# Row scales of the two MLPs: TensorE matmuls and a ScalarE copy, or a write to scratch memory and a broadcast read

## What is computed

```python
def rms_norm(x, g):
    xf = x.astype(jnp.float32)
    y = xf * lax.rsqrt(jnp.mean(xf * xf, axis=-1, keepdims=True) + EPS)
    return (y * g.astype(jnp.float32)).astype(x.dtype)

def squared_relu_mlp(h, w_up, w_down):
    a = jax.nn.relu(h @ w_up)
    return (a * a) @ w_down

# for each layer l: first the mixer, then
        x = x + squared_relu_mlp(rms_norm(x, mlp_norm[l]), w_up[l], w_down[l])
```

## Time and profile before

| | us |
|---|---|
| median of 3 runs (1101.26 to 1101.33) | 1101.28 |
| the profiled execution, its own time | 1101.01 |
| its span in the trace | 1099.2 |
| PE busy | 1091.1 (99%) |
| DVE busy | 782.8 (71%) |
| ACT busy | 479.4 (44%) |
| POOL busy | 77.3 (7%) |
| share of the DMA engines in weight loads (queue 1) | 31.4% |

### The profile page before, as it was taken

The page is one execution under the profiler, slowest core; times in us unless marked ns, Lnnn a source line. Parts: engine busy times, 40 slices in busy tenths (PEclk is TensorE's granted clock), DMA queues, the critical chain, the costliest instruction groups (busy, mean ns, idle before and its releaser), DMA issues.

```text
span 1099.2 us, 13443 instructions
## 1 busy us (share of the span) xinstructions
PE 1091.1 (99%) x5168; PEld 900.2 (82%) x5168; DVE 782.8 (71%) x980; ACT 479.4 (44%) x695; POOL 77.3 (7%) x58
## 2 busy tenths in 40 slices
PE   8999999999999999999999999999999999999998
PEld 7888888888888888888888877788888888888887
DVE  4765554787787787788764489965678678678686
ACT  7221234354354353354542367855444344344342
POOL 0000012000000000001430032103000000000000
PEclk9999999999999999999999999999999999999999
DMA  7433463314415315301232201044314314314202
GB/s 192 102 91 101 136 208 96 107 47 154 115 40 159 109 38 170 99 1 39 97 115 96 95 22 39 2 168 140 96 58 138 112 58 146 104 58 152 78 1 77
DMA packets 144752, 105.90 MB, mean 96 GB/s; under 512 B 12592, under 2 KB 121136, under 8 KB 144688
## 3 DMA queue, kind: packets, MB, share of 16 engines
q1 hardware_dynamic: 143648, 105.03, 31.4%
q10 hardware_dynamic: 1040, 0.00, 0.1%
HBM read 102.93 MB, written 2.10 MB: 96 GB/s over the span
## 4 chain that ended last, share of the span: by engine, by line
PE 98%; DMA 1%; ACT 1%; DVE 0%; issue 0%; SPq 0%; ACTq 0%; DVEq 0%
PE ps L603 32%; PE ps L630 28%; PE ps L490 20%; PE ps L692 10%; PE ps L717 2%; PE ps L756 2%; PE ps L779 2%; PE ps L768 1%; DMA kv<-in_x 1%; PE ps L759 1%; PE ps L572 0%; PE ps L666 0%; PE ps L585 0%; PE ps L737 0%; PE ps L791 0%
## 5 line engine op out<-in xcount | busy, mean ns | idle before, releaser
L603 PE MATMUL ps<-h,w_hi 128*128 128x512 f32 x1024 | 316.3, 390 | 0.0
L630 PE MATMUL ps<-w_hi,h 128*128 128x512 f32 x896 | 277.7, 389 | 0.0
L603 PEld LDWEIGHTS ps<-h,w_hi 128*128 128x128 f32 x1024 | 191.6, 188 | 39.2
L603 PE MATMUL ps<-h,w_lo 128*128 128x512 f32 x512 | 199.5, 390 | 0.0
L630 PEld LDWEIGHTS ps<-w_hi,h 128*128 128x128 f32 x896 | 168.2, 188 | 34.9
L490 PE MATMUL ps<-h,w_hi 128*128 128x512 f32 x608 | 187.9, 390 | 0.0
L630 PE MATMUL ps<-w_lo,h 128*128 128x512 f32 x448 | 174.4, 389 | 0.0
L969 ACT ACTIVATE w_hi<-b_raw 128x1024 fp32r<-128x1024 f32 x80 | 82.0, 1054 | 141.5 <-PE ps L603 81.9
L490 PEld LDWEIGHTS ps<-h,w_hi 128*128 128x128 f32 x608 | 113.7, 188 | 23.4
L490 PE MATMUL ps<-h,w_lo 128*128 128x512 f32 x304 | 118.4, 390 | 0.0
L1305 DVE TENSOR_TENSOR w_lo<-b_raw,w_hi 128x1024 fp32r<-128x1024 f32 x80 | 95.9, 1223 | 26.4 <-ACT w_hi L969 26.4
(11 more groups left out here) (136 smaller groups left out, 1201.8 us busy)
## 6 DMA issues: line engine op xcount, KB each, us to landing
b_raw<-in_w_down SPq DMA_DIRECT2D x64, 512.0 KB, 4.5
w_raw<-in_w_up SPq DMA_DIRECT2D x64, 512.0 KB, 4.0
w_raw<-in_a_w_in SPq DMA_DIRECT2D x23, 512.0 KB, 3.7
w_raw<-in_w_kv SPq DMA_DIRECT2D x16, 512.0 KB, 3.7
w_raw<-in_a_w_out SPq DMA_DIRECT2D x8, 512.0 KB, 4.1
w_raw<-in_w_q SPq DMA_DIRECT2D x8, 512.0 KB, 3.5
w_raw<-in_w_o SPq DMA_DIRECT2D x8, 512.0 KB, 4.2
kv<-in_x SPq DMA_DIRECT2D x4, 512.0 KB, 6.4
```

Source lines behind the costliest of these rows:

```text
L603: last = nc.tensor.matmul(ps[:, v % 4, :], w[:, s_, k * P:(k + 1) * P], h_of[inp][:, half, k, :], start=(k == 0 and i == 0), stop=(k == KC ...
L630: last = nc.tensor.matmul(ps[:, CHAIN[p][tb], :], op[half][:, k, tb * P:(tb + 1) * P], w[:, s_, cols], start=(FRESH[p] and k == 0 and i == ...
```

## The change

For the two MLPs, steps 3 and 4 become two transfers, both issued by ACT:

- `scales_out`: ACT waits for POOL's `rcol` and issues a DMA that writes the 512 scales to a 2 x 512 scratch tensor in DRAM, one float at a time, in token order.
- `scales_in`: ACT waits until that write has landed and issues a DMA that reads the 2 KB row into each of the 128 partitions of `rB` (256 KB).
- DVE's first `rectified` waits for that read. DVE's `lo(q, 3)`, which stood behind it, goes ahead of the wait.
- PE's `norm_spread` for the MLPs is gone. The wait by which `down_product` 2 kept bank 6 from being overwritten too early is now on `nms` instead of on `rB`.

The first mixer's norm keeps its matmuls and its copy.

```diff
@@ PE, down_product @@
                     elif p == 2:
-                        pe.wait_ge(s_rB, 3 if q else 2)
+                        pe.wait_ge(s_nms, (NORM_M1 if q else NORM_M0) + 1)
@@ PE, mlp @@
                             if j == 0:
                                 norm_sums((NORM_M0, NORM_M1)[layer])
-                            if j == 1:
-                                norm_spread((NORM_M0, NORM_M1)[layer])
@@ ACT @@
+            def scales_out(layer):
+
+                act.wait_ge(s_nrc, (NORM_M0, NORM_M1)[layer] + 1)
+                with nc.allow_non_contiguous_dma(reason="row scales: one float a token"):
+                    act.dma_start(scales[layer, :].rearrange("(t p) -> p t", p=P),
+                                  rcol[:, (NORM_M0, NORM_M1)[layer], :]).then_inc(s_rput, 16)
+
+            def scales_in(layer):
+
+                act.wait_ge(s_rput, 16 * (layer + 1))
+                act.dma_start(rB[:], scales[layer:layer + 1, :].to_broadcast([P, T])).then_inc(s_rgot, 16)
@@ ACT, mlp @@
+                        if q % NQ == 0 and j == 1:
+                            scales_out(layer)
                         if j < 6:
                             hi(q, j + 2)
                         else:
                             hi(q, j + 3)
                         if q % NQ == 0 and j == 1:
-                            row_scales(2 + layer)
+                            scales_in(layer)
@@ DVE, mlp @@
                         if q % NQ == 0 and j == 1:
-                            dve.wait_ge(s_rB, 2 + layer)
+                            lo(q, 3)
+                            dve.wait_ge(s_rgot, 16 * (layer + 1))
                         if j:
                             rectified(q, j - 1)
                         elif q % NQ:
                             add_pair(q - 1, 6)
-                        if j < 6:
+                        if j >= 6:
+                            lo(q, j + 3)
+                        elif q % NQ or j != 1:
                             lo(q, j + 2)
-                        else:
-                            lo(q, j + 3)
```

More of the change, by code:

```diff
@@ L130, in build @@
 def build(nc, x, a_norm, a_w_in, a_conv, a_w_out, kv_norm, w_kv, k_norm, b_norm, w_q, q_norm,
-          lam_q1, lam_k1, lam_q2, lam_k2, sub_norm, w_o, mlp_norm, w_up, w_down, out):
+          lam_q1, lam_k1, lam_q2, lam_k2, sub_norm, w_o, mlp_norm, w_up, w_down, out, scales):
     with ExitStack() as ctx:
@@ L243, in build @@
         s_rB = sem("s_rB")
+        s_rput = sem("s_rput")
+        s_rgot = sem("s_rgot")
         s_mix = sem("s_mix")
@@ L1728 @@
     out = nc.dram_tensor("out_x", (1, T, D), F32, kind="ExternalOutput").ap()
-    build(nc, *args, out)
+    scales = nc.dram_tensor("row_scales", (2, T), F32, kind="Internal").ap()
+    build(nc, *args, out, scales)
     r = run_bass_kernel_spmd(nc, [arrays], core_ids=[0])
```

## The result

The changed kernel takes **1113.29 us** (median of 5 runs, 1112.29 to 1113.69) against 1101.27 for the kernel before: 12.0 us or 1.07% more, ratio 1.0107 with an interval of 1.0096 to 1.0119. I had forecast 1099.5 and no change to speak of, with a range up to 1102.5. What happened is what the prediction named as the sign of being wrong, PE idle before unit 4 and a transfer of over 5 us, at a larger size than any rival's; and, as the runs show, it came mainly through the write and not, as the slow rival had it, through the read.

The account below looks back on a forecast made before the run. PE bounds the kernel, holding 98% of the chain; removing its spread saves 1.8 us and the transfers, 6.9 us against 9.1 and 11.4, stay hidden: 1101.28 - 1.8 = 1099.5 us, range 1098.9 to 1102.5.

Parts of the forecast that it names:

- the slow rival: Broadcast read into `rB` takes 11.9 us at 28 GB/s; PE waits in both layers, 1108.8 us; chance 0.15.
- PE's spread, 1.8 us: Removing PE's `norm_spread` from its path at both MLP starts saves 1.8 us, ends 1.78 and 2.3.
- The row of work and the budget: DVE's work up to slab 4's `lo` before unit 4 leaves the transfers 9.1 us (layer 0) and 11.4 (layer 1) free.
- R: Moment `rB` is complete in a layer; may be as late as 204.0 us in layer 0, 784.1 in layer 1.
- w + r: Write plus read of the scales, each from issue to landing: forecast 6.9 us, hidden in both layers.
- the formula: Before unit 4, PE pays one to one for transfer time over 9.1 us in layer 0 and 11.4 in layer 1.
- w = 3.0, ends 2.0 and 5.0: Time for the write of 512 single floats to DRAM to land: 3.0 us, between 2.0 and 5.0.
- r = 3.9: Time for the read of the 2 KB row into 128 partitions to land: 3.9 us, ends 2.0 and 11.9.
- the weight load started early by the moved `lo`: Slab 5's load may start near 197.7 us beside the read and cost it no more than 1.5 us.
- Two more DMAs ... cost PE nothing: Two added transfers on a queue that carried one so far were claimed to cost PE nothing.
- The clock: PE's clock might also fall if PE waits as long as in the slow read; no size given.
- the copy ahead of unit 4's transposes: In layer 1, ACT's copy behind its second wait would end near 3 us after `rB` is complete, in time.

Follow-up runs that it names:

- e7: Kernel before without PE's spread, ACT's copy or any transfer for the two MLPs, DVE using left-over scales: 1099.47 us.
- e10: Changed kernel with the write in 16 B pieces, slab 4 made ahead of the wait, and one reordering ACT copy per layer: 1099.61 us.
- e2: Changed kernel with useless matmuls filling PE's waits before unit 4 in both layers: 1109.45 us.
- the probes: Two kernels equal to the one before, plus unused transfers on SyncE in attention, one after another; each ran once, only transfer times read from the trace.
- e1: Changed kernel with the write as 128 pieces of 16 B, order put right in DVE's read of `rB`: 1100.79 us.
- e5: Changed kernel with the 16 B write, PE's sums taking every fourth token so that the row is in token order: 1101.5 us.
- e3: Changed kernel with both halves of slab 4 made ahead of the wait for the scales, slow write kept: 1109.0 us.
- e6: e5 with both halves of slab 4 also made ahead of the wait: 1101.12 us.
- e9: Changed kernel with the 16 B write, ACT writing MLP-norm squares in order of tokens in fours, slab 4 ahead of the wait: 1101.08 us.
- e4: Kernel before with the write of 512 single floats added on ACT and used by nobody: 1101.27 us.

## Why the prediction was wrong

- **PE's spread, 1.8 us: right.** e7 measured 1.77, e10 1.69.
- **The row of work and the budget: right.** "4.68 us after R": R was 210.03 and slab 4's `lo` ended at 213.50 + 1.22 = 214.72, 4.69 later. w + r of 15.1 against the budget of 9.1 gives 6.0 us; unit 4 began 5.1 + 0.9 us after the 208.9 or so at which it could have. In layer 1 the formula gives 4.0 and the starts 4.1. e2, without the clock's part, confirms it over both layers (7.8 to 8.2 against 8.1 measured).
- **The step that failed: w = 3.0, ends 2.0 and 5.0.** I took the price of a single-float write from loads of single floats and from a bulk store. Both were true of themselves (in the probes, reading 512 single floats took 2.1 us and writing the scales in 16 B pieces 1.4), and neither has the property that counts: floats written side by side. It was 10.1 and 9.6 us. With these w and the prediction's r of 3.9 the waits would have been 4.9 + 2.1 = 7.0 us of the 10.0. The slow-read rival mentioned a write of single floats that takes 8 us in one sentence and gave it no chance of its own. With no row that writes small pieces to DRAM, the upper end should not have come from rows that read.
- **r = 3.9: fair in size, wrong in reason.** It was 5.0 and 5.8, and since the write had used up the budget this cost the other 3.0 us of waiting. The suspicion that the earlier trace rows showed a slow broadcast fell: alone, the 2 KB row took 3.1 us and the 256 B row 3.0, against 2.7 for different rows, and so the prediction's remark that this trace agrees with one place in DRAM holding reads back is not borne out either. What lengthened it was, in all likelihood, the weight load started early by the moved `lo`, for which I had allowed up to 1.5 us. Against the 3.1 us alone, it took 1.9 to 3.0 us more with one load beside it (5.0 to 6.1 in the changed kernel, e1, e2 and e5), and 3.1 to 5.4 more with two (6.2 to 8.5 in e3, e6, e9 and e10).
- **"Two more DMAs ... cost PE nothing": right, but not for their neighbours.** The load of slab 5, issued while the slow write was under way, took 11.6 us to land in the changed kernel and 6.2 in e4, instead of 4.0. Beside the 16 B write and the read of e1 it took 5.9.
- **The clock: left open, and it was a third of the loss.** I said that a gap of 5 us "might" lower it and put no price on it. e2 prices it at 3.4 to 3.8 us: after the waits PE ran at its lower level for several microseconds. The Trainium skill ("TensorE: Matmul & The Clock Gate", section What's actually happening) says that the engine's default is the low level and that activity releases it; the trace agrees, 0.73 and 0.52 in the stretches behind the waits and 1.00 there with the waits filled.
- **The order in layer 1:** the copy ahead of unit 4's transposes, which I had called in time, was PE's first wait there (2.3 us), because the round trip was 8.5 us longer than assumed. It changed no sum: slab 4 came later still.
- **Within the forecast's terms** the measured w and r give 1099.5 + 6.0 + 4.0 = 1109.5, and e2's 3.8 on top gives the measured 1113.3. That last step is no check, since the 3.8 is a difference to the same run; the starts of matmuls give 3.9 on their own.

## What to carry to other kernels

A transfer that is new to a kernel is priced from a row with the same direction and the same spacing at its destination; where no row has it, the range must be wide enough for a factor of four, or the transfer is to be measured alone first, which takes one run. Write small results to DRAM in contiguous pieces of 16 B or more and repair the order once, on an engine that has time, not in each of the instructions that use it. And where a wait may reach a TensorE that never waited before, add what the lower clock costs behind it: here 3.8 us on 9.3 us of waiting.

## What was unexpected of the hardware

- 128 single floats written side by side to DRAM took 7.7 to 8.1 us, 512 of them 8.8, 32 of them 3.6, pairs 3.2; the same 128 floats 16 B or 64 B apart took 1.4 and 1.5 us, and 512 floats as 128 pieces of 16 B 1.4. The Trainium skill ("DMA: Bandwidth & Descriptors", section Specifications) says that pieces under 512 B are read, modified and written. If that were the whole price, 16 B pieces and spread floats would be slow as well, and they are not; the measurement decides.
- Such a write slows what shares the DMA engines, though these are nearly idle (0.03 in the probe): a 512 KB load beside it took 11.6 us instead of 4.0, and 5.9 beside the same bytes in 16 B pieces.
- Stepping through floats costs each engine that does it half as much again or twice as much. With reads 16 B apart PE's eight weight loads and matmuls took 1.65 us instead of 0.79, ACT's 128x512 copy 1.11 instead of 0.60 and DVE's multiplication, one operand of two, 1.05 instead of 0.69; with writes 512 B apart ACT's square took 1.13 instead of 0.62. The Trainium skill ("SBUF — State Buffer", section Door 1: The DMA port swizzle) gives lines of 16 B, where each access that goes to a new line pays; the four measurements here, with steps of 16 B or more, agree.
- After 3.6 us of waiting in two pieces, layer 1 ran longer at the low clock than layer 0 after 5.7 us in one (2.5 us lost against 1.4). Why is open.
